# Norm weights in a transfer of their own, small rows turned inside the second unit, norm sums a quarter into it, and keep-warm matmuls at the token load

## What is computed

```python
def rms_norm(x, g):
    var = jnp.mean(x * x, axis=-1, keepdims=True)
    return x * lax.rsqrt(var + EPS) * g

for i in range(2):
    n = rms_norm(h, norm_mix[i])
    z = n @ w_in[i]                                  # 1024 -> 7 x 1024
    xa, ya, xb, g_post, g_pre, m_a, m_b = split(z)
    ua = causal_dwconv(xa, ca0[i], conv_a_w[i]) + conv_a_b[i]        # width 4
    out_a = (rg_lru(ua, ...) * gelu(ya)) @ w_a_out[i]
    ub = causal_dwconv(g_pre * xb, cb0[i], conv_b_w[i])              # width 3
    out_b = (g_post * ub) @ w_b_out[i]
    h = h + (sigmoid(m_a) * out_a + sigmoid(m_b) * out_b) @ w_o[i]
    n2 = rms_norm(h, norm_ffn[i])
    h = h + (swiglu(n2) if i == 0 else moe_top2_of_8(n2))
    h = h + sigmoid(rms_norm(h, norm_ple[i]) @ w_ple_gate[i]) * (p[i] @ w_ple_proj[i])
y = rms_norm(h, final_norm)
```

## Time and profile before

| | us |
|---|---|
| median of 3 runs | 1192.95 |
| the runs | 1192.92 to 1193.67 |
| profiled execution | 1193.82 |
| its span, first to last instruction | 1192.1 |

### The profile page before, as it was taken

The page is one execution under the profiler, slowest core; times in us unless marked ns, Lnnn a source line. Parts: engine busy times, 40 slices in busy tenths (PEclk is TensorE's granted clock), DMA queues, the critical chain, the costliest instruction groups (busy, mean ns, idle before and its releaser), DMA issues.

```text
span 1192.1 us, 27219 instructions
## 1 busy us (share of the span) xinstructions
PE 1153.6 (97%) x11887; PEld 928.4 (78%) x11887; DVE 875.0 (73%) x977; ACT 645.4 (54%) x664; POOL 26.8 (2%) x60
## 2 busy tenths in 40 slices
PE   6999999999999999999999996999999999999998
PEld 4888888888888888788888884877767767777466
DVE  4986896878766668995987766977686676866465
ACT  5665744466454446666564445855556455554242
POOL 4000001000000001000001000000000000000000
PEclk8999999999999999999999998999999999999999
DMA  9565566555665654366576546999999999999501
GB/s 282 171 221 201 176 212 205 189 177 177 211 197 190 207 183 158 121 210 213 163 229 198 179 177 253 381 408 398 375 393 372 390 382 370 407 374 333 185 1 37
DMA packets 171067, 289.30 MB, mean 243 GB/s; under 512 B 5195, under 2 KB 132187, under 8 KB 170954
## 3 DMA queue, kind: packets, MB, share of 16 engines
q1 hardware_dynamic: 169040, 283.20, 67.2%
q0 software_dynamic: 1728, 4.16, 1.1%
q10 hardware_dynamic: 202, 0.51, 0.2%
HBM read 286.53 MB, written 1.52 MB: 242 GB/s over the span
## 4 chain that ended last, share of the span: by engine, by line
PE 85%; DVE 9%; ACT 3%; issue 1%; DMA 1%; ACTq 0%; DVEq 0%
PE acc L546 15%; PE acc L548 14%; PE acc L547 14%; PE aux L914 14%; PE acc L901 5%; PE acc L899 5%; PE acc L900 5%; DVE wl L1431 2%; PE acc L538 2%; PE acc L531 2%; PE acc L532 2%; PE aux L844 1%; PE aux L712 1%; PE aux L690 1%; DVE xb L1551 1%
## 5 line engine op out<-in xcount | busy, mean ns | idle before, releaser
L546 PE MATMUL acc<-xn,wh 128*128 128x264 f16 x1280 | 354.0, 277 | 2.4 <-ACT xa L1030 0.9
L547 PE MATMUL acc<-xn,wh 128*128 128x264 f16 x1280 | 354.1, 277 | 0.0
L548 PE MATMUL acc<-xn,wl 128*128 128x264 f16 x1280 | 354.1, 277 | 0.0
L1431 DVE SCALAR_TENSOR_TENSOR wl<-raw,wh 128x2048 f16<-128x2048 f32 x124 | 283.4, 2289 | 93.4 <-ACT wh L986 93.1
L986 ACT ACTIVATE wh<-raw 128x2048 f16<-128x2048 f32 x124 | 235.6, 1903 | 0.0
L901 PE MATMUL acc<-ga,wl 128*128 128x96 f16 x1536 | 199.5, 206 | 0.6 <-issue 0.6
L900 PE MATMUL acc<-ga,wh 128*128 128x96 f16 x1536 | 199.5, 206 | 0.3 <-issue 0.3
L899 PE MATMUL acc<-ga,wh 128*128 128x96 f16 x1536 | 199.5, 206 | 0.0
L1437 DVE SCALAR_TENSOR_TENSOR wl<-raw,wh 128x2048 f16<-128x2048 f32 x64 | 144.3, 2288 | 58.9 <-ACT wh L995 58.9
L995 ACT ACTIVATE wh<-raw 128x2048 f16<-128x2048 f32 x64 | 122.1, 1911 | 100.8 <-PE acc L901 97.0
L900 PEld LDWEIGHTS acc<-ga,wh 128*128 128x128 f16 x1536 | 150.3, 98 | 7.8 <-issue 7.6
(11 more groups left out here) (306 smaller groups left out, 1735.7 us busy)
## 6 DMA issues: line engine op xcount, KB each, us to landing
raw<-in_moe_w_gu SPq DMA_DIRECT2D x64, 1024.0 KB, 10.4
raw<-in_w_in SPq DMA_DIRECT2D x56, 1024.0 KB, 5.1
raw<-in_ffn_w_gu SPq DMA_DIRECT2D x24, 1024.0 KB, 5.2
sa<-in_moe_w_gu SPq DMA_DIRECT2D x16, 1024.0 KB, 9.5
xb<-in_moe_w_gu SPq DMA_DIRECT2D x16, 1024.0 KB, 11.0
raw<-in_ffn_w_dn SPq DMA_DIRECT2D x12, 1024.0 KB, 5.1
ya<-in_moe_w_dn SPq DMA_DIRECT2D x10, 1024.0 KB, 7.6
sg<-in_moe_w_dn SPq DMA_DIRECT2D x10, 1024.0 KB, 7.3
```

The costliest lines, as they stand in the source:

```text
L546: nc.tensor.matmul(bank, hi, x[:, 0, x0 + k, :], start=(k == 0), stop=False)
L547: nc.tensor.matmul(bank, hi, x[:, 1, x0 + k, :], start=False, stop=False)
L548: last = nc.tensor.matmul(bank, lo, x[:, 0, x0 + k, :], start=False, stop=(k == k_chunks - 1))
L1431: op(V.scalar_tensor_tensor(out=wl[:, s, 0:size], in0=raw_slot[s][:, 0:size], scalar=WS, in1=wh[:, s, 0:size], op0=ALU.mult, op1=ALU.subtr ...
```

## The change

- **Start.** The norm weights of the mixers (`norm_mix`, the first of the thirteen small transfers) count on a semaphore of their own, `gain_loaded`. TensorE does six keep-warm matmuls, turns these two rows in eight small transposes (`first_gains`), does six more keep-warm matmuls, transposes all token chunks without a stop, and then does ten keep-warm matmuls. ScalarE makes `hx` of four chunks before `hi(0)`.
- **Small rows.** The other rows are turned inside slice 1, behind its first 12 of 48 matmuls; ScalarE copies them there.
- **Norm sums.** In all three early matrices the ones matmul stands behind the first 12 matmuls of the second slice, and the last sum of the squares goes to a buffer of its own.
- **Low halves.** In both mixers and the FFN a second low half is made ahead of the norm, and the low half in the conv turns is that of the next slice: `lo(n0 + u + 5)`. In the last slice before an early matrix the low half moves behind the last residual add.
- **Embeddings.** All their transposes are 128 x 128; the unused rows are cleared first, and a DMA on GpSimd's queue waits for that.

```diff
@@ TensorE, unit
-                    if between and m == 0:
-                        between()
+                        if between and (m, k) == (0, C // 2 - 1):
+                            between()
@@ TensorE, early_matrix
-                early_unit(n, turn, early_stats if stats == 0 else None)
+                early_unit(n, turn)
                 for u in range(1, SEC):
-                    unit(n + u, u, u % 2, hx, C, 256, between=early_stats if stats == u else None)
+                    unit(n + u, u, u % 2, hx, C, 256, between=between if u == 1 else None)
...
+            def first_stats():
+                small_rows()
+                early_stats()
...
+            def first_gains():
+                pe.wait_ge(gain_loaded, 16)
+                bank = aux_bank()
+                for c in range(C):
+                    last = nc.tensor.transpose(bank[:, c * LAYERS:(c + 1) * LAYERS], vrows[0:LAYERS, c * P:(c + 1) * P],
+                                               ident[0:LAYERS, 0:LAYERS])
+                last.then_inc(aux_full, 1)
...
-            keep_warm(8)
+            keep_warm(6)
+            first_gains()
+            keep_warm(6)
             pe.wait_ge(x_loaded, 48)
             samples_in_full()
             pe.wait_ge(h_out, C)
+            keep_warm(10, aux[:, 3, :])
...
-                early_matrix(n0, 2 * l, 0 if l else 1)
+                early_matrix(n0, 2 * l, early_stats if l else first_stats)
@@ ScalarE, start
-            small_rows()
-            act.wait_ge(g16_ready, 2)
-            hi(0)
+            nc.scalar.activation(g16[:, :, 0:LAYERS], aux_bank()[:, 0:C * LAYERS].rearrange("p (c r) -> p c r", c=C),
+                                 ACT.Copy, scale=XS).then_inc(aux_done, 1)
+            act.wait_ge(aux_done, AX_GAIN)
             for c in range(C):
+                if c == 4:
+                    hi(0)
                 act.wait_ge(h_out, c + 1)
                 hx_high(c, 0)
@@ ScalarE, mixer
-                    if u == 1 - l:
+                    if u == 1:
+                        if l == 0:
+                            small_rows()
                         stats()
                     if u > 0 or l:
                         evac(n0 + u, xa[:, 2 * u:2 * u + 2, 3:3 + T])
-                    if u == 1 - l:
+                    if u == 1:
                         norm_hi()
+                        act.wait_ge(aux_done, AX_VEC)
                     if u:
                         first_tap(u - 1)
@@ ScalarE, FFN
+                if u == 1:
+                    stats()
                 if u == 0:
-                    stats()
+                    act.wait_ge(sq_ready, 3 * 2)
...
-                if u == 0:
+                if u == 1:
                     norm_hi()
@@ VectorE, fold
-                    op(V.tensor_tensor(sq[:, 0, :], sq[:, 0, :], sq[:, 1, :], ALU.add), sq_ready, 3)
+                    op(V.tensor_tensor(rtmp[:], sq[:, 0, :], sq[:, 1, :], ALU.add), sq_ready, 3)
@@ VectorE, mixer
                 if l == 0:
                     lo(2)
+                lo(n0 + LEAD)
+                lo(n0 + LEAD + 1)
+                if l == 0:
                     lambdas()
-                lo(n0 + LEAD)
                 norm(v("norm_mix", l))
...
                     op(V.tensor_tensor(xa[:, s, 3:3 + T], xa[:, s, 3:3 + T], by_rstd(), ALU.mult), xa_scaled)
-                    lo(n + u + 1 + LEAD)
+                    lo(n + u + 2 + LEAD)
                     vec_e.wait_ge(tap_ready, SEC * l + u + 1)
                     conv(ua, xa, 4, row, bias, u)
...
-                    if u < SEC - 1:
-                        lo(n + u + 1 + LEAD)
+                    if u < SEC - 2:
+                        lo(n + u + 2 + LEAD)
...
-                    if not late:
+                    if not late and (l or u < SEC - 1):
                         lo(n + u + LEAD)
...
                             last_to_early(n + u, plain_add, LAYERS)
+                            lo(n + u + LEAD)
@@ VectorE, embedding gate
-                    if n + u + LEAD < N_END:
+                    if n + u + LEAD < N_END and (l or u < SEC - 1):
                         lo(n + u + LEAD)
...
                             last_to_early(n + u, gated_add, 1)
+                            lo(n + u + LEAD)
@@ VectorE, FFN
             lo(N_GU + LEAD)
+            lo(N_GU + LEAD + 1)
             norm(v("norm_ffn", 0))
             for u in range(SEC):
-                if u < SEC - 1:
-                    lo(N_GU + u + 1 + LEAD)
                 evacuated(N_GU + u)
                 x = (pair_u if u % 2 else pair_g)[:, u // 2]
                 op(V.tensor_tensor(x, x, by_rstd(), ALU.mult), dv if u % 2 else g_scaled)
+                if u < SEC - 2:
+                    lo(N_GU + u + 2 + LEAD)
```

More of the change, by code:

```diff
@@ L259, in program @@
         N_CONST = 13 + NE
-        AX_VEC = 2
+        AX_GAIN = 1
+        AX_VEC = AX_GAIN + 2
         AX_P = AX_VEC + 1 + LAYERS * PC
@@ L442, in _ @@
                 pool.dma_start(prows[:, l, 1, :], a["p_prompt"][l, 0, P:2 * P, :]).then_inc(p_loaded, 16)
+                if l == 0:
+                    pool.wait_ge(x_clear, 2)
                 pool.dma_start(prows[0:NSAMP, l, 2, :], a["p_sample"][l, :, 0, :]).then_inc(p_loaded, 16)
@@ L548, in unit, with early_unit @@
                         last = nc.tensor.matmul(bank, lo, x[:, 0, x0 + k, :], start=False, stop=(k == k_chunks - 1))
+                        if between and (m, k) == (0, C // 2 - 1):
+                            between()
                     if last_unit and m == 0:
                         last.then_inc(tile_mm, 1)
-                    if between and m == 0:
-                        between()
                 last.then_inc(unit_mm, 1)
-            def early_unit(n, turn, between=None):
+            def early_unit(n, turn):
                 if n >= 2:
@@ L574, in early_unit, with early_matrix @@
                                                         start=False, stop=(j == C - 1))
-                    if between and k == C - 3:
-                        between()
                 last.then_inc(unit_mm, 1)
-            def early_matrix(n, turn, stats):
-                early_unit(n, turn, early_stats if stats == 0 else None)
+            def early_matrix(n, turn, between):
+                early_unit(n, turn)
                 for u in range(1, SEC):
-                    unit(n + u, u, u % 2, hx, C, 256, between=early_stats if stats == u else None)
+                    unit(n + u, u, u % 2, hx, C, 256, between=between if u == 1 else None)
             def matrix(n, x, ready=None, base=0, before_norm=False):
@@ L615, in early_stats @@
                 pe.wait_ge(sq_ready, 3 * k + 3)
-                nc.tensor.matmul(bank[:, 0:T], ones[:], sq[:, 0, :], start=True, stop=True).then_inc(aux_full, 1)
+                nc.tensor.matmul(bank[:, 0:T], ones[:], rtmp[:], start=True, stop=True).then_inc(aux_full, 1)
+            def first_stats():
+                small_rows()
+                early_stats()
             def norm_stats(warm=18, router=None):
@@ L634, in norm_stats @@
                     keep_warm(warm)
-            def columns(bank, src, c):
-                nc.tensor.transpose(bank[:, 0:P], src[:, 0, c * P:(c + 1) * P], ident[:])
-                nc.tensor.transpose(bank[:, P:2 * P], src[:, 1, c * P:(c + 1) * P], ident[:])
-                return nc.tensor.transpose(bank[:, SEQ:T], src[0:NSAMP, 2, c * P:(c + 1) * P], ident[0:NSAMP, 0:NSAMP])
             def samples_in_full():
@@ L669, in embeddings @@
                     for c in range(PC):
-                        columns(aux_bank(), prows[:, l], c).then_inc(aux_full, 1)
+                        bank = aux_bank()
+                        for t in range(3):
+                            last = nc.tensor.transpose(bank[:, t * P:(t + 1) * P], prows[:, l, t, c * P:(c + 1) * P],
+                                                       ident[:])
+                        last.then_inc(aux_full, 1)
             pe.wait_ge(const_ready, N_FIRST)
-            keep_warm(8)
+            keep_warm(6)
+            first_gains()
+            keep_warm(6)
             pe.wait_ge(x_loaded, 48)
@@ L717, in _ @@
             mixer(0)
-            early_matrix(N_GU, 1, 0)
+            early_matrix(N_GU, 1, early_stats)
             pe.wait_ge(xn_ready, 4 * 2)
@@ L1064, in small_rows @@
             def small_rows():
-                r_mix, r_ffn = v("norm_mix"), v("norm_ffn")
+                r_ffn = v("norm_ffn")
                 for g in range(2):
@@ L1069, in small_rows @@
                     cs = slice(4 * g, 4 * g + 4)
-                    nc.scalar.activation(g16[:, cs, 0:LAYERS], rows_in[:, :, r_mix:r_mix + LAYERS], ACT.Copy, scale=XS)
                     nc.scalar.activation(g16[:, cs, LAYERS:LAYERS + 1], rows_in[:, :, r_ffn:r_ffn + 1], ACT.Copy,
-                                         scale=XS).then_inc(g16_ready, 1)
+                                         scale=XS)
```

(2 more changed lines are left out.)

8 lines of the change are left out of this document (3 added, 5 removed).

## The result

The changed kernel takes 1207.7 us (median of four, 1205.4 to 1209.05), the kernel before 1193.31 beside it (one of its four executions took 1819.89 us, the others 1192.92 to 1193.67): a ratio of 1.012, 95% interval 1.010 to 1.014, 14.4 us slower. 20.4 us were forecast. The direction holds; the time lies 0.3 us under the low end of the range. The profiled execution took 1205.4 us (span 1203.7, against 1192.1), so its record has to account for +11.6 us, 8.8 less than forecast; 7.0 of these 8.8 turned out to have nothing to do with the steps of the forecast.

A forecast was written before the change was run, and what follows sets the result against it. TensorE, busy nearly throughout, was taken as the bound, with VectorE and ScalarE a chain of their own. First mixer +13.05, FFN -2.0, second mixer +9.4 gave +20.4 us: 1214.2 profiled, median 1213.4, range 1208 to 1218.

The forecast's parts named there:

- The conv turns: Mixers' first turns: VectorE's low half waits for ScalarE's high half behind the tap; a turn is 8.6 us, 3.05 longer.
- Mixer 1: Second mixer: same longer turns, two more low halves ahead of the norm; slice 88 starts at 539.2 against 529.8, +9.4 us.
- Mixer 0: First mixer: 10.85 us from the longer turns plus 2.2 from the later first scaling, +13.05 us.
- slow restart of slice 7: First mixer: half clock for one 3.5 us stretch behind a gap of 3 us, 1.75 us, making slice 7 7.05 us.
- The forecast's 11.3: First mixer's loss in us if slice 7 stays at full clock, instead of 13.05.
- FFN: Dense FFN's early matrix loses a 1.3 us wait for the norm sum and a 0.7 us eviction wait: -2.0 us.
- The front: Kernel start: steps moved earlier but hidden behind the first weight slice landing at 17.2 us; zero gain.
- second rival: Kernel start: first slice lands earlier, first scaling up to 3.6 us sooner, 1209.8 us; chance 0.10.
- The transposes in slice 1: Small-row transposes moved between slice 1's matmuls: price of a slow stretch 0 to 1.75 us, taken as 0.
- The slow slice: Second slice running slow because transposes do not count as busy for the clock; norm sum some 0.2 us more.
- The sum: Whole kernel: 13.05 - 2.0 + 9.4 = +20.4 us on the profiled 1193.82, 1214.2; median 1213.4.
- the moving front: Kernel start: first weight slice lands earlier than the row says, 1209.8 us; chance 0.10.

The follow-up runs named there:

- low halves back: Changed kernel with both mixers' first turns back to one low half ahead of the norm and the earlier low-half order: 1186.6 us, ratio 0.9932.
- low halves later: Kernel before with, in mixer 0 alone, two low halves ahead of the norm and each turn's low half one slice further ahead: 1207.2 us, ratio 1.0104.
- high half ahead: Changed kernel with ScalarE's high half put ahead of the first tap in both mixers' first turns: 1183.7 us, ratio 0.9912.
- the one without the branch: Changed kernel without TensorE's branch on the routing flag and its overflow path: 1208.56 us, ratio 1.0105.
- the run that undid it: Changed kernel with its edits in the FFN's first turn undone (norm sums, second low half, low-half order): 1212.9 us, ratio 1.0162.
- hold: GpSimd's early loads wait for four high halves: on the changed kernel with ScalarE's high half ahead of the tap 1179.06 us, on the kernel before 1191.96.
- the best version: Changed kernel with ScalarE's high half ahead of the tap and GpSimd's early loads held until four high halves are made: 1179.06 us, ratio 0.9885.

## Why the prediction was right, and where it failed

- **The conv turns: right to a tenth.** Forecast from the first scaling on: slices at +4.37, +13.0, +23.2 and +33.3; measured +4.43, +13.04, +23.28 and +33.42. Mixer 1: slice 87 at +30.7, measured +30.78. The mechanism is shown by three runs (low halves back, low halves later, high half ahead). TensorE waits ahead of slices 4 and 84 too, which the forecast did not list, though it had the time of their start: TensorE came to them sooner.
- **Mixer 0: 13.05 forecast, 12.1 measured.** The mis-sized term is the slow restart of slice 7: that stretch had 1.00 in the profiled execution (TensorE had waited 1.95 us), and 0.58 in the one without the branch (3.22 us). The forecast's 11.3 for the full clock is the case that came true, plus 0.4 at the first scaling and 0.4 at slice 7 (0.1 in its start, 0.3 in its length). The restart falls differently from one execution to the next.
- **Mixer 1: 9.4 forecast, 9.5 measured. FFN: -2.0 forecast, -2.4 measured**, 2.1 by the run that undid it.
- **The front: zero gain, but not for the reason given.** The earlier trace rows was read as a fixed landing at 17.2 us. It is none: the first high half began at 15.19 in the changed kernel's record and at 16.9 to 19.5 in the other records with its front and no hold. By the forecast's own test ("the first low half comes before 17 us" against 17.14) it just holds. The gain was taken back by the landings of slices 1, 3 and 4, for which ScalarE waited until 21.84, 29.41 and 32.29, so the norm began at 36.62, where 34.05 + 2.2 was forecast:
```profile
15.19 1.91 ACT L1000 ACTIVATE wh<-raw 128x2048 f16<-128x2048 f32 x1 [3.46 <-DMA raw<-in_w_in]
32.29 1.91 ACT L1000 ACTIVATE wh<-raw 128x2048 f16<-128x2048 f32 x1 [0.97 <-DMA raw<-in_w_in]
```
  That later slices land behind the first was the forecast's own argument against its second rival. But the zero is in part luck, a gain and a loss that cancel in this record: with the low halves back, so without lo(4) ahead of it, the first scaling came at 46.90, against 43.73 in the kernel before. The reason named, that the load queue is not touched, missed that other queues share the DMA engines.
- **The transposes in slice 1: no price, as taken.** TensorE had clock 1.00 from 27 to 30 us, through the eight transposes at 28.3. The Trainium skill, TensorE: Matmul & The Clock Gate, section Part 4: PE-mode transpose, says that transposes do not count as busy for the clock in the way that matmuls do. The slow slice that the prediction worked out from it is not seen behind these eight.
- **The sum: the step that failed.** "Beside the start, these are all that the moved steps can win" left out the longest single wait on the list it was read from, and so put any change of it at nothing, with no reason given:
```profile
PE aux L844 <- issue: 6.4, 1, 6.4
```
  No part of the change touches the gathers. But the change adds 22 matmuls to TensorE's stream, 44 instructions with their weight loads, and that moved the branch and its target to a place where it does not stall: 22.8 us from logits to experts became 15.8, so -7.0. With it the forecast would have been 1213.4 - 7.0 = 1206.4, against the median of 1207.7. No row of the kernel before told that the wait would go; that it is long and ends on nothing that the profile shows was there to read, and would have made a rival. The rival nearest in number, the moving front at 1209.8, is not what happened.
- **From the record to the median.** The profiled execution is the fastest of its four. Where the first slice lands, and whether slices 7 and 87 restart at half clock, differ from one execution to the next and move it by 1 to 3 us each, as the records of two close kernels suggest (without the keep-warm matmuls 1208.65 us, first high half at 16.93; without the branch 1209.86 us, 17.99 and slice 7 at 0.58). That these make the whole spread was only argued.

## What to carry to other kernels

When a producer is asked for one item more ahead, look at what stands before that item in the producer's own queue: if it waits for the asker, the two engines take turns, and one order or the other must be turned with it (here 24 us between the two orders of ScalarE). Read every long wait on the bounding engine, "issue" too, even where the change has no edit: a wait behind a branch can hang on how many instructions stand ahead of it, and any added or removed instruction may give or take it (seen here at one branch). Before moving work to an earlier place at the start of a kernel, look at who shares the DMA engines with the first loads.

## What the runs showed of the hardware

- A branch on TensorE took 5.96 to 6.65 us or 0.34 to 0.79, by its place in the code: 22.0 to 23.2 us against 15.8 to 16.6 over the same work, with 0 and 256 instructions more ahead of it (stall) and with 25 and 44 more (none). The 48 gathers behind it took 3.9 to 4.0 us with the stall, at a granted clock of 0.50 to 0.54, and 2.5 without, at 1.00.
- Waits that are already met are not free on TensorE: 212 instructions of two waits each filled 11.4 to 34.2 us, 0.11 us each.
- With all DMA engines busy, 1.3 MB from GpSimd's queue cost the first weight slice 4.8 us in the two records compared: 214 to 254 GB/s with it, 341 to 349 without. From 15 to 18 us the weights' queue moved 0.19 MB with it and 1.05 MB without. Why less is moved in all while it runs was not tried.
- Idle time alone did not tell the clock of the next slice: 0.50 behind 4.68 us, 0.58 behind 3.22, 0.61 behind 2.05 (slice 86 of the changed kernel), but 1.00 behind 3.27 (slice 0 of the best version) and 3.20 (slice 84 of the changed kernel).
